# A two-block transformer step in fp32: cross attention and mLSTM sums of squares as high and low fp32r products of a pair added on VectorE

## The chip, the cores and the metric

The program runs on one NeuronCore of a Trainium2 chip. The metric is device time in microseconds (us) for one launch, input and output transfers between the chip's memory and the core included. Three runs of the kernel before gave 1216.65, 1218.11 and 1218.13 us; the median, 1218.11 us, is the time before.

## The reference

Two blocks, batch 1, 256 tokens, width 1024, all in fp32. The first block has three branches on one normalised input: a stick-breaking attention with 8 heads of 128, an mLSTM with 4 heads of 256 (short causal convolution, SiLU, a gated linear recurrence in parallel form), and a cross attention with 4 heads of 256 against 256 memory tokens. Gates mix them, then comes a ReLU-squared MLP. The second block has dilated attention, an SSM and another MLP. The two pieces of it that the change touches are root-mean-square norms over one head's 256 channels:

```
def _rmsnorm(x, g):
    xf = x.astype(jnp.float32)
    y = xf * lax.rsqrt(jnp.mean(xf * xf, axis=-1, keepdims=True) + EPS)
    return (y * g.astype(jnp.float32)).astype(x.dtype)

# cross attention, per head of 256
qn = _rmsnorm(q, gq); kn = _rmsnorm(mk, gk)
# mLSTM, per head of 256
hm = _rmsnorm(hm, ml_norm_g[l].reshape(ML_HEADS, 1, ML_HD))
y_ml = (_merge_heads(hm) * jax.nn.sigmoid(ml_o.astype(jnp.float32))).astype(dt)
```

## The kernel before

Activations lie turned: channels in the 128 partitions, the 256 tokens in the free dimension. All weights (over 200 MB) stream from memory once, in *units* of 1024 x 256. A unit's raw fp32 tile has one of three slots. ScalarE (ACT) rounds it to a high half `w_hi` (L203), VectorE (DVE) subtracts to get the low half `w_lo` (L209), and TensorE (PE) multiplies in the one-pass format fp32r: high by high, high by low, low by high (L241), 48 products of 128x128 by 128x256 for a unit, 24 for each half of its outputs. A unit can't begin on PE before its `w_lo` is written (semaphore `w_split`), and `w_hi` of a slot can't be overwritten before PE has finished the unit that was there.

There is no scheduler. The order of work on each engine is written out by hand, engine by engine, and each engine runs its instructions strictly in that order, with waits on semaphores between engines. So the attention work of a head (the "thread" of small operations) is interleaved by hand with the units.

A head of 256 channels is two tiles. Its sum of squares over channels is a sum over partitions, taken by PE as a product of a 128x128 matrix of ones with the squares, which puts the sum in every partition. These products are plain fp32 (through `mm`, L1618). In the profile one fp32 product shows as two records.

*Cross attention* has four heads. In pass i (1 to 4) PE computes the first half of the key unit, then `cross_sums` for head i-1, then the second half, half the query unit, `cross_logits`, and so on. `c_sq` holds four tiles of squares, two of k and two of q, written by ACT (L520 for k, L540 for q). DVE adds each pair into one tile (`cross_pair`, L1098); PE makes one fp32 product with ones for k and one for q; ACT turns the sums into inverse roots (`inv_rms`, L445 and L446), DVE scales (L1110), PE makes the logits.

*mLSTM* has four heads, and for i = 1 to 3 a pass of four units q, k, v, o. On PE: unit q, scores of head i-1, unit k, half of unit v, values of head i-1, the other half, half of unit o, `mlstm_sums` of head i-1 (two fp32 products with ones, one for each tile of squares), the other half of unit o. ACT runs, in this order: the square of the head's output (L637), `inv_rms` on the sums (L445, L446), the copy of unit v out of PSUM (L455), a table load and the SiLU of the *next* head (L621), the `w_hi` of a unit (L203), the sigmoid gate (L642), a table load (L450), the output's high half (L647), the copy of unit o, another `w_hi`. DVE runs: two `w_lo`, the divide of head i-1 (L1225 to L1229), the convolution of head i (L1198, three groups of four operations, each group waiting for the one before), the scaling with the inverse root (L1235), a `w_lo`, the gate product (L1241), the output's low half (L992), a `w_lo`, the decay weights and scores of head i (L1211 to L1219), a copy of unit k (L982). The fourth head's small operations lie among the units of the stage that follows, `gx` (eight units, L690 its gates).

Chains between the engines that matter below: DVE's convolution, then ACT's SiLU, then ACT's `w_hi`, then DVE's `w_lo`, then the next PE unit.

Of the kernel before, what the change touches and what calls it, by code (L numbers as in the profile page):

```python
# [8 lines left out]
FP32 = mybir.dt.float32  # L9
FP32R = mybir.dt.float32r  # L10
ALU = mybir.AluOpType
ACT = mybir.ActivationFunctionType
AXX = mybir.AxisListType.X

P = 128
T = 256
# [37 lines left out]
H0, M0, Y0 = 0, 8, 16  # L54
H2, M2 = M0, H0
YSB, YML, YX = Y0, Y0 + 8, Y0 + 16
# [41 lines left out]
def build(nc, a, out):  # L98

    ctx = ExitStack()  # L100
    with ctx:
# [5 lines left out]
        def S(name):  # L107
            if name not in sems:
                sems[name] = ctx.enter_context(nc.semaphore(name))
            return sems[name]  # L110
# [6 lines left out]
        x_hi = sb("x_hi", [P, OPND, T], FP32R)  # L117
        x_lo = sb("x_lo", [P, OPND, T], FP32R)
# [3 lines left out]
        ident, ones, later = (cst[:, n * P:(n + 1) * P] for n in range(3))  # L122
# [21 lines left out]
        def bank(b, *dims):  # L144
            v = ps[:, b, :]
            if len(dims) == 3:
                return v[:, 0:dims[0] * dims[1] * dims[2]].rearrange("p (a b c) -> p a b c", a=dims[0], b=dims[1])
            if len(dims) == 2:
                return v[:, 0:dims[0] * dims[1]].rearrange("p (a b) -> p a b", a=dims[0])
            return v[:, 0:dims[0]]  # L150
# [5 lines left out]
        def rows(t, at, n):  # L156
            return t[:, at:at + n, :]

        def need(eng, name, n):

            if n > 0:
# [10 lines left out]
        n_hi, n_lo = (v[:, M0:M0 + 3, :].rearrange("p a b -> p (a b)").rearrange("p (h c) -> p h c", h=2)  # L172
                      for v in (x_hi, x_lo))
        ones_r, later_r = (x_hi[:, M0 + 3, n * P:(n + 1) * P] for n in range(2))
        dtc, acs = (small[:, n:n + 64].rearrange("p (t h) -> p t h", t=2) for n in (256, 320))
        skip = tab[:, 40 * KT:40 * KT + 16]
        dtb, a_log = (tab[0:32, n:n + 1] for n in (40 * KT + 16, 40 * KT + 17))
# [127 lines left out]
        def conv_tiles(i):  # L305
            return [2 * i, 2 * i + 1, 2 * i + 8, 2 * i + 9]
# [131 lines left out]
        def _(act):  # L438
            ahead = iter(range(len(FILLED)))
            chain = Chain(act, S("act_chain"))  # L440
# [30 lines left out]
            def early_hi(u):  # L471

                next(ahead)
                for n in (0, 4):
                    act.wait_ge(S(f"w_early{u}_{n}"), 16)
                    A(w_hi[:, u, n:n + 4], raw[:, u, n:n + 4], ACT.Copy)\
                        .then_inc(S(f"w_hi{u}_half" if n == 0 else f"w_hi{u}"), 1)
# [9 lines left out]
                A(rows(x_hi, H0 + 2 * b, 2), mix[:, 2 * b:2 * b + 2], ACT.Copy).then_inc(S("xn_hi"), 1)  # L487

            early_hi(0)
            act.wait_ge(S("eps"), 1)  # L490
            act.wait_ge(S("mem_ss"), 1)
            inv_rms(mem_row, bank(6, T), D).then_inc(S("mem_rs"), 1)
# [476 lines left out]
        def _(dve):  # L969
# [125 lines left out]
            def cross_pair(j, n):  # L1095

                dve.wait_ge(S("c_sq"), 2 * j + n + 1)
                tt(c_sq[:, 2 * n], c_sq[:, 2 * n], c_sq[:, 2 * n + 1], ALU.add).then_inc(S("c_pair"), 1)  # L1098

            cross_pair(0, 0)  # L1100

# [87 lines left out]
                low(2 * (i - 1) + YSB, bank(7, 2, T), "y_hi", i + 4, "y_lo")  # L1189


            def conv(pad, dst, name, tiles, stride):

                for m in range(1, 4):
                    if m > 1:
                        chain(last)
                    for n in range(4):
                        last = stt(dst[:, n], pad[:, n, m:m + T], pc("conv_w" + name, tiles[n] + stride * m),  # L1198
                                   dst[:, n], ALU.mult, ALU.add)
                return last  # L1200

            def mlstm_conv(i):

                dve.wait_ge(S("rnn_c0"), i + 1)
                conv(m_qkp, m_cv, "", conv_tiles(i), 16).then_inc(S("rnn_cv"), 1)

            def mlstm_weights(j):

# [63 lines left out]
            def gated(stage, i, first, n=None, splits=2):  # L1272

                for _ in range(splits):
                    split()
                u = U(stage, i, 1, 2)
                dst = rows(mix, 2 * i, 2)
                evacuated(dve, u - 1)
                finished(dve, u)
                tt(gt, gt, unit_bank(u), ALU.mult).then_inc(taken(u), 1)  # L1280
                evacuated(dve, u)
                if first:
                    V.tensor_copy(dst, gt).then_inc(S("p_used"), 1)
                else:
                    tt(dst, dst, gt, ALU.add).then_inc(S("p_used"), 1)
                if n is not None:
                    low(2 * i + M0, dst, "mix_hi", n, "mix_lo")
# [3 lines left out]
            mlstm_scores(3)  # L1291
            gated("gx", 1, True)
            mlstm_divide(3)
            gated("gx", 2, True)
            mlstm_scale(3)
            mlstm_gate(3)
            gated("gx", 3, True)
# [316 lines left out]
        def _(pe):  # L1614
            FP, TOK = False, True

            def mm(o, l, r, start=True, stop=True):
                return nc.tensor.matmul(o, l, r, start=start, stop=stop)  # L1618
# [9 lines left out]
            def half(u, o, at, tok=FP, nk=KT, lo=None):  # L1628

                if o == 0:  # L1630
                    begin(u)
                last = products(pe, u, o, at, tok, nk, lo=lo)
                if o == 1:
                    last.then_inc(S(f"unit{u % SLOTS}"), 1)

            def unit(u, at, tok=FP, nk=KT, lo=None):
                half(u, 0, at, tok, nk, lo)
                half(u, 1, at, tok, nk)
# [76 lines left out]
            def cross_sums(j):  # L1715

                pe.wait_ge(S("c_pair"), 2 * j + 2)
                for n in range(2):
                    last = mm(bank(3, 2, T)[:, n], ones, c_sq[:, 2 * n])
                last.then_inc(S("c_ss"), 1)  # L1720

            def cross_logits(j):
# [22 lines left out]
                last.then_inc(S("soft_y"), 1)  # L1745

            pe.wait_ge(S("cst_in"), 16)
            for i in range(1, 5):
                k, q, v = (U("cross", i, n, 3) for n in range(3))
                mem, x = (M0, YSB) if i < 4 else (H0, H0)  # L1750
                if i == 4:
                    pe.wait_ge(S("xn_lo"), 4)
                half(k, 0, mem)
                cross_sums(i - 1)
                if i == 4:
                    gate_sums()
                half(k, 1, mem)
                half(q, 0, x)
                cross_logits(i - 1)
                half(q, 1, x)  # L1760
                half(v, 0, mem, TOK)
                cross_turn(i - 1)
                half(v, 1, mem, TOK)
                if i == 4:
                    gate_columns()
                cross_values(i - 1)
# [62 lines left out]

            def mlstm_sums(j):  # L1830

                pe.wait_ge(S("rnn_sq"), j + 1)
                for d in range(2):
                    last = mm(bank(6, T), ones, m_sq[:, d], d == 0, d == 1)
                last.then_inc(S("rnn_ss"), 1)

            q, k, v, o = (U("mlstm", 0, n, 4) for n in range(4))
            half(q, 0, H0)
# [7 lines left out]
            for i in range(1, 4):  # L1846
                q, k, v, o = (U("mlstm", i, n, 4) for n in range(4))
                unit(q, H0)
                mlstm_scores(i - 1)
                unit(k, H0)  # L1850
                half(v, 0, H0, TOK)
                mlstm_values(i - 1)
                half(v, 1, H0, TOK)
                half(o, 0, H0)
                mlstm_sums(i - 1)
                half(o, 1, H0)

            def gated(stage, i, at, nk=KT, h=H0):

                unit(U(stage, i, 0, 2), h)  # L1860
                unit(U(stage, i, 1, 2), at, FP, nk)
# [330 lines left out]
```

## Time and profile before

| what | value |
|---|---|
| median of three runs | 1218.11 us (1216.65 to 1218.13) |
| the profiled execution's own time | 1217.88 us |
| its span, first to last instruction | 1216.1 us |
| PE busy | 1203.7 us, 99% |
| DVE busy | 814.0 us, 67% |
| ACT busy | 672.5 us, 55% |
| mean data rate from memory | 173 GB/s |
| cross attention passes on PE | about 30 to 124 us |
| mLSTM passes on PE | about 186 to 296 us, `gx` to about 347 us |

Matmuls overlap in the records, so that a product's own duration is longer than the step from one to the next. The time that a product costs PE is read from the starts of the records. A busy share near 100% says that PE seldom stops; it doesn't say that nothing else decides where it stops. For that there is the chain of waits, which follows the work that ended last back from its end.

### The profile page before, as it was taken

What the parts mean: (1) busy time and instruction counts of PE and PEld (TensorE: products, weight loads), DVE (VectorE), ACT (ScalarE), POOL (GpSimd) and SP (SyncE); (2) the same over time, 40 slices, a digit from 0 to 9 for tenths busy, and PEclk for the clock granted to TensorE, in tenths of its full rate; (3) what the DMA queues carried; (4) which work ended last, traced back from release to release, by engine and by line L of the source; (5) the groups of instructions that cost most, each with busy time, mean ns of one, the idle gap of its engine ahead of it and who ended that gap; (6) DMA issues with size and microseconds to landing.
All of it is one profiled execution on the core that took longest, in us unless ns stands there. A gap on an engine that the chain in (4) does not pass through costs nothing.

```text
span 1216.1 us, 21663 instructions
## 1 busy us (share of the span) xinstructions
PE 1203.7 (99%) x9458; PEld 1169.4 (96%) x9458; DVE 814.0 (67%) x913; ACT 672.5 (55%) x801; POOL 11.0 (1%) x24
## 2 busy tenths in 40 slices
PE   9999999999999999999999999999999999999998
PEld 8999999999999999999999999999999998999886
DVE  7866676777655566776447658888885457777543
ACT  7643545676544444554344558889876345555442
POOL 0000000000000000000000000000000000000000
PEclk9999999999999999999999999999999999999999
DMA  9543445555655554556565546556455564455651
GB/s 326 171 157 105 143 151 163 152 148 158 193 184 183 179 170 156 179 193 218 174 190 179 177 129 202 174 171 194 148 176 163 191 208 139 156 174 181 235 190 53
DMA packets 202494, 210.75 MB, mean 173 GB/s; under 512 B 6540, under 2 KB 191244, under 8 KB 202400
## 3 DMA queue, kind: packets, MB, share of 16 engines
q1 hardware_dynamic: 199712, 200.30, 51.9%
q0 software_dynamic: 2112, 8.17, 2.4%
q8 instruction: 75, 1.23, 0.4%
q10 hardware_dynamic: 576, 0.90, 0.2%
q14 instruction: 19, 0.16, 0.0%
HBM read 208.25 MB, written 1.09 MB: 172 GB/s over the span
## 4 chain that ended last, share of the span: by engine, by line
PE 91%; DVE 4%; ACT 4%; DMA 1%; issue 1%; DVEq 0%; ACTq 0%
PE ps L241 73%; PE ps L2111 7%; PE ps L1618 6%; DVE w_lo L209 2%; PE ps L1667 1%; ACT w_hi L203 1%; PE ps L1621 1%; DVE arena L1198 1%; PE ps L2071 1%; PE ps L250 1%; DMA arena<-rows 0%; DMA pcol<-in_params 0%; PE ps L2078 0%; ACT L642 0%; DVE arena L1227 0%
## 5 line engine op out<-in xcount | busy, mean ns | idle before, releaser
L241 PE MATMUL ps<-x_hi,w_hi 128*128 128x256 f32 x2448 | 702.2, 287 | 0.5 <-DVE w_lo L209 0.4
L241 PE MATMUL ps<-x_hi,w_lo 128*128 128x256 f32 x2448 | 692.6, 283 | 0.0
L241 PE MATMUL ps<-x_lo,w_hi 128*128 128x256 f32 x2448 | 692.5, 283 | 0.0
L209 DVE TENSOR_TENSOR w_lo<-raw,w_hi 128x2048 fp32r<-128x2048 f32 x187 | 427.5, 2291 | 228.9 <-ACT w_hi L203 228.9
L241 PEld LDWEIGHTS ps<-x_hi,w_hi 128*128 128x128 f32 x2448 | 469.4, 192 | 4.9 <-issue 3.4
L241 PEld LDWEIGHTS ps<-x_lo,w_hi 128*128 128x128 f32 x2448 | 469.5, 192 | 0.8
L241 PEld LDWEIGHTS ps<-x_hi,w_lo 128*128 128x128 f32 x2448 | 469.3, 192 | 0.0
L203 ACT CAST w_hi<-raw 128x2048 fp32r<-128x2048 f32 x187 | 354.3, 1900 | 118.1 <-PE ps L241 73.8
L1618 PE MATMUL ps<-arena 128*128 128x256 f32 (+5 forms) x432 | 66.0, 340 | 1.3 <-ACT arena L843 1.3
L241 PE MATMUL ps<-w_hi,x_hi 128*128 128x256 f32 x224 | 64.3, 287 | 0.0
L241 PE MATMUL ps<-w_lo,x_hi 128*128 128x256 f32 x224 | 63.3, 283 | 0.0
L241 PE MATMUL ps<-w_hi,x_lo 128*128 128x256 f32 x224 | 63.3, 283 | 0.0
L1198 DVE SCALAR_TENSOR_TENSOR arena<-arena,pcol 128x256 f32<-128x256 f32 x144 | 60.2, 480 | 3.5 <-ACT arena L607 2.7
L1618 PEld LDWEIGHTS ps<-arena 128*128 128x128 f32 (+2 forms) x432 | 52.9, 170 | 8.5 <-ACT arena L843 1.5
L764 ACT ACTIVATE arena<-ps 128x512 f32<-128x512 f32 x30 | 17.9, 598 | 77.6 <-PE ps L241 77.6
L2111 PE MATMUL ps<-w_hi,x_hi 128*128 128x512 f32 x128 | 49.8, 389 | 0.0
L2111 PE MATMUL ps<-w_hi,x_lo 128*128 128x512 f32 x128 | 49.8, 389 | 0.0
L2111 PE MATMUL ps<-w_lo,x_hi 128*128 128x512 f32 x128 | 49.8, 389 | 0.0
L1356 DVE TENSOR_TENSOR arena<-arena 128x512 f32<-128x512 f32 x32 | 22.1, 692 | 31.9 <-ACT arena L764 31.9
L241 PEld LDWEIGHTS ps<-w_hi,x_lo 128*128 128x128 f32 x224 | 42.9, 191 | 0.0
L241 PEld LDWEIGHTS ps<-w_hi,x_hi 128*128 128x128 f32 x224 | 42.9, 191 | 0.0
L241 PEld LDWEIGHTS ps<-w_lo,x_hi 128*128 128x128 f32 x224 | 42.9, 191 | 0.0
(233 smaller groups left out, 960.3 us busy)
## 6 DMA issues: line engine op xcount, KB each, us to landing
raw<-in_w_in SPq DMA_DIRECT2D x170, 512.0 KB, 4.6
raw<-in_w_ff SPq DMA_DIRECT2D x64, 512.0 KB, 4.5
raw<-in_w_up SPq DMA_DIRECT2D x32, 512.0 KB, 4.7
raw<-in_w_down SPq DMA_DIRECT2D x32, 512.0 KB, 4.4
raw<-in_w_mem_kv SPq DMA_DIRECT2D x16, 512.0 KB, 5.7
raw<-in_w_out SPq DMA_DIRECT2D x16, 512.0 KB, 4.9
raw<-in_w_ssm_proj SPq DMA_DIRECT2D x16, 512.0 KB, 4.7
raw<-in_w_x_proj SPq DMA_DIRECT2D x8, 512.0 KB, 4.6
```

The costliest lines, as they stand in the source:

```text
L203: nc.scalar.copy(w_hi[:, s], raw[:, s]).then_inc(S(f"w_hi{s}"), 1)
L209: nc.vector.tensor_tensor(w_lo[:, s], raw[:, s], w_hi[:, s].bitcast(FP32), ALU.subtract)\
L241: last = nc.tensor.matmul(dst, l, r, start=start and k == 0 and m == 0, stop=stop and k == nk - 1 and m == 2)
L250: last = nc.tensor.matmul(dst, wt[:, c], xt[:, at + k, :], start=k == 0 and m == 0, stop=k == KT - 1 and m == 2)
L764: A(f, unit_bank(u), ACT.Relu).then_inc(taken(u), 1)
L1198: last = stt(dst[:, n], pad[:, n, m:m + T], pc("conv_w" + name, tiles[n] + stride * m), dst[:, n], ALU.mult, ALU.add)
L1356: chain(tt(q, f, bc(rs_row(), 2), ALU.mult))
L1618: return nc.tensor.matmul(o, l, r, start=start, stop=stop)
L1621: return nc.tensor.transpose(o, i, ident[0:i.shape[0], 0:i.shape[0]])
L1667: last = nc.tensor.matmul(dst, l, r, start=kind == 0 and k == 0, stop=kind == 2 and k == KT - 1)
L2071: nc.tensor.matmul(dst, wt[:, u % SLOTS, k, o * P:(o + 1) * P], x_hi[:, H0 + k, :], start=k == 0 and m == 0, stop=False)
L2111: last = nc.tensor.matmul(y_bank(c, t), xt[:, U0 + 4 * (b % 8) + k, t * P:(t + 1) * P], wide(wt[:, u % SLOTS])[:, k], start=b % 8 == 0 and ...
```

## The change

In both places DVE now produces one tile for a pair of squares and splits it into an fp32r high half and an fp32r low half, kept in rows of `x_hi` and `x_lo` that are free at that time, and PE multiplies each half with ones in fp32r.

- Cross attention: `cross_pair` has three dependent operations (add, cast, subtract) where it had one. `cross_sums` has four fp32r products where it had two fp32 ones. The ones in fp32r are written by ACT near the program's start.
- mLSTM: a new `mlstm_pair` (add, cast, subtract) on DVE, placed between the first and the second group of the next head's convolution; for the fourth head it stands between the two `w_lo` of the third pair of `gx`. `mlstm_sums` has two fp32r products where it had two fp32 ones, and stands behind the whole unit o, where it stood between its halves.

```diff
+        c_hi, c_lo = (rows(v, YML, 2) for v in (x_hi, x_lo))
+        m_hi, m_lo = (v[:, M0 + 4, :] for v in (x_hi, x_lo))
+        ones_c = x_hi[:, YML + 4, 0:P]
...
             early_hi(0)
+            act.wait_ge(S("ones"), 1)
+            A(ones_c, ones, ACT.Copy).then_inc(S("ones_c"), 1)
...
             def cross_pair(j, n):
                 dve.wait_ge(S("c_sq"), 2 * j + n + 1)
-                tt(c_sq[:, 2 * n], c_sq[:, 2 * n], c_sq[:, 2 * n + 1], ALU.add).then_inc(S("c_pair"), 1)
+                chain(tt(c_sq[:, 2 * n], c_sq[:, 2 * n], c_sq[:, 2 * n + 1], ALU.add))
+                chain(V.tensor_copy(c_hi[:, n], c_sq[:, 2 * n]))
+                tt(c_lo[:, n], c_sq[:, 2 * n], c_hi[:, n].bitcast(FP32), ALU.subtract).then_inc(S("c_pair"), 1)
...
-            def conv(pad, dst, name, tiles, stride):
+            def conv(pad, dst, name, tiles, stride, between=None):
                 for m in range(1, 4):
                     if m > 1:
                         chain(last)
+                    if m == 2 and between is not None:
+                        between()
...
+            def mlstm_pair(j):
+                dve.wait_ge(S("rnn_sq"), j + 1)
+                chain(tt(m_sq[:, 0], m_sq[:, 0], m_sq[:, 1], ALU.add))
+                chain(V.tensor_copy(m_hi, m_sq[:, 0]))
+                tt(m_lo, m_sq[:, 0], m_hi.bitcast(FP32), ALU.subtract).then_inc(S("m_pair"), 1)
...
-                conv(m_qkp, m_cv, "", conv_tiles(i), 16).then_inc(S("rnn_cv"), 1)
+                conv(m_qkp, m_cv, "", conv_tiles(i), 16, (lambda: mlstm_pair(i - 1)) if i else None)\
+                    .then_inc(S("rnn_cv"), 1)
...
             mlstm_divide(3)
-            gated("gx", 2, True)
+            split()
+            mlstm_pair(3)
+            gated("gx", 2, True, splits=1)
...
                 pe.wait_ge(S("c_pair"), 2 * j + 2)
                 for n in range(2):
-                    last = mm(bank(3, 2, T)[:, n], ones, c_sq[:, 2 * n])
+                    mm(bank(3, 2, T)[:, n], ones_c, c_hi[:, n], True, False)
+                    last = mm(bank(3, 2, T)[:, n], ones_c, c_lo[:, n], False, True)
                 last.then_inc(S("c_ss"), 1)
...
             def mlstm_sums(j):
-                pe.wait_ge(S("rnn_sq"), j + 1)
-                for d in range(2):
-                    last = mm(bank(6, T), ones, m_sq[:, d], d == 0, d == 1)
-                last.then_inc(S("rnn_ss"), 1)
+                pe.wait_ge(S("m_pair"), j + 1)
+                mm(bank(6, T), ones_r, m_hi, True, False)
+                mm(bank(6, T), ones_r, m_lo, False, True).then_inc(S("rnn_ss"), 1)
...
                 half(v, 1, H0, TOK)
-                half(o, 0, H0)
+                unit(o, H0)
                 mlstm_sums(i - 1)
-                half(o, 1, H0)
```

On DVE, in the first mLSTM pass, from the divide to the scaling, the instructions stand like this in the kernel before (`arena` is the scratch tile, `pcol` holds the convolution's weights, the waits are semaphores):

```order
L1229 TENSOR_TENSOR arena<-ps,arena 128x512 [waits rnn_num,dve_chain]
L1198 SCALAR_TENSOR_TENSOR arena<-arena,pcol 128x256 [waits rnn_c0]
L1198 SCALAR_TENSOR_TENSOR arena<-arena,pcol 128x256 x3
L1198 SCALAR_TENSOR_TENSOR arena<-arena,pcol 128x256 [waits dve_chain]
L1198 SCALAR_TENSOR_TENSOR arena<-arena,pcol 128x256 x3
L1198 SCALAR_TENSOR_TENSOR arena<-arena,pcol 128x256 [waits dve_chain]
L1198 SCALAR_TENSOR_TENSOR arena<-arena,pcol 128x256 x3
L1235 SCALAR_TENSOR_TENSOR arena<-arena,pcol 128x256 [waits rnn_r]
```

The same stretch of DVE in the changed kernel, whose line numbers are a little higher:

```order
L1246 TENSOR_TENSOR arena<-ps,arena 128x512 [waits rnn_num,dve_chain]
L1207 SCALAR_TENSOR_TENSOR arena<-arena,pcol 128x256 [waits rnn_c0]
L1207 SCALAR_TENSOR_TENSOR arena<-arena,pcol 128x256 x3
L1214 TENSOR_TENSOR arena<-arena 128x256 [waits rnn_sq,dve_chain]
L1215 CAST x_hi<-arena 128x256 [waits dve_chain]
L1216 TENSOR_TENSOR x_lo<-arena,x_hi 128x256 [waits dve_chain]
L1207 SCALAR_TENSOR_TENSOR arena<-arena,pcol 128x256 x4
L1207 SCALAR_TENSOR_TENSOR arena<-arena,pcol 128x256 [waits dve_chain]
L1207 SCALAR_TENSOR_TENSOR arena<-arena,pcol 128x256 x3
L1252 SCALAR_TENSOR_TENSOR arena<-arena,pcol 128x256 [waits rnn_r]
```

The add, the cast and the subtract stand between the first and the second group, and each of the three waits for the one before it. The second group waits for nothing new, but stands behind them in the queue.

On DVE, in the first cross attention pass, between the q tile's pair and the logits' reduction, the changed kernel has these rows (before, the first three were one `TENSOR_TENSOR`, L1098):

```order
L1103 TENSOR_TENSOR arena<-arena 128x256 [waits c_sq]
L1104 CAST x_hi<-arena 128x256 [waits dve_chain]
L1105 TENSOR_TENSOR x_lo<-arena,x_hi 128x256 [waits dve_chain]
L212 TENSOR_TENSOR w_lo<-raw,w_hi 128x2048 [waits w_hi1]
L212 TENSOR_TENSOR w_lo<-raw,w_hi 128x2048 [waits w_hi2]
L1117 SCALAR_TENSOR_TENSOR arena<-arena,pcol 128x256 [waits c_r]
```

Two `w_lo` and the scaling for the logits are behind the longer pair.

## Rows read from the trace of the kernel before

**Rows 1.** The page's first part: busy time, share and instructions by engine.
```profile
PE 1203.7 (99%) x9458; PEld 1169.4 (96%) x9458; DVE 814.0 (67%) x913; ACT 672.5 (55%) x801; POOL 11.0 (1%) x24
```
**Rows 2.** Chain that ended last, mLSTM stage: start us, us, what.
```profile
237.02 0.88 PE ps L1618 x4
...
263.42 1.59 DVE arena L1198 x4
...
266.74 1.69 DVE arena L1198 x4
...
294.56 1.68 DVE arena L1198 x4
...
306.95 2.30 DVE w_lo L209
309.39 11.74 PE ps L241 x96
...
335.48 115.19 PE ps L241 x960
```
**Rows 3.** Timeline of PE, second cross pass: start us, us, engine, line, what.
```profile
54.63 1.03 PE L1618 MATMUL ps<-arena,cst 128*128 128x256 f32 x4
55.31 0.47 PE L241 MATMUL ps<-x_hi,w_hi 128*128 128x256 f32 x1
55.62 0.28 PE L241 MATMUL ps<-x_lo,w_hi 128*128 128x256 f32 x1
```
**Rows 4.** DVE's copies into tile mix: line, count, duration ns min/median/max.
```profile
L1283 DVE COPY mix<-arena x8: 427/427/428, 313.8 to 930.1; 128x512 f32<-128x512 f32 x8
```
**Rows 5.** Timeline of DVE, first and second cross pass.
```profile
31.02 0.84 DVE L1098 TENSOR_TENSOR arena<-arena 128x256 f32<-128x256 f32 x2
...
36.18 1.67 DVE L1110 SCALAR_TENSOR_TENSOR arena<-arena,pcol 128x256 f32<-128x256 f32 x4
...
53.84 0.42 DVE L1098 TENSOR_TENSOR arena<-arena 128x256 f32<-128x256 f32 x1 [0.56 <-ACT arena L540]
```
**Rows 6.** Timeline of PE, first cross pass: the sums, then the logits.
```profile
32.63 1.03 PE L1618 MATMUL ps<-arena,cst 128*128 128x256 f32 x4
...
39.24 1.89 PE L1618 MATMUL ps<-arena 128*128 128x256 f32 x8
```
**Rows 7.** Timeline of PE, mLSTM: first sums, next key unit, third sums.
```profile
236.86 1.03 PE L1618 MATMUL ps<-arena,cst 128*128 128x256 f32 x4
...
247.58 0.36 PE L241 MATMUL ps<-x_hi,w_hi 128*128 128x256 f32 x1
...
291.95 1.13 PE L1618 MATMUL ps<-arena,cst 128*128 128x256 f32 x4 [0.40 <-ACT arena L637]
```
**Rows 8.** Timeline of ACT, first mLSTM pass, from the norm to the SiLU.
```profile
237.93 0.47 ACT L445 ACTIVATE arena<-ps,small 128x256 f32<-128x256 f32 x1 [2.40 <-PE ps L1618]
...
239.36 1.28 ACT L621 ACT_TABLE_LOAD   x1
240.65 1.06 ACT L621 ACTIVATE arena<-arena 128x1024 f32<-128x1024 f32 x1
```
**Rows 9.** Timeline of DVE, mLSTM passes.
```profile
231.47 0.42 DVE L1225 SCALAR_TENSOR_TENSOR arena<-ps,arena 128x256 f32<-128x256 f32 x1
231.93 0.42 DVE L1226 TENSOR_TENSOR arena<-arena,ps 128x256 f32<-128x256 f32 x1
...
243.61 2.29 DVE L209 TENSOR_TENSOR w_lo<-raw,w_hi 128x2048 fp32r<-128x2048 f32 x1 [2.96 <-ACT w_hi L203]
...
263.34 5.08 DVE L1198 SCALAR_TENSOR_TENSOR arena<-arena,pcol 128x256 f32<-128x256 f32 x12
```
**Rows 10.** PE's waits: line, for whom, us in total, times, longest.
```profile
PE ps L2071 <- ACT x_hi L939: 2.9, 1, 2.9
```
**Rows 11.** Busy time after that wait: window, PE, PEld, DVE, ACT, POOL, granted clock, DMA share, GB/s.
```profile
1026.00:1030.00 4.00, 3.74 (x19) 3.77 (x20) 4.00 (x12) 3.08 (x7) 0.00 (x0) 0.58 0.09 30
```
**Rows 12.** Chain that ended last, same place: start us, us, what.
```profile
1026.26 3.41 PE ps L2071 x16
```

More of the change, by code:

```diff
@@ L1747, in _ @@
             pe.wait_ge(S("cst_in"), 16)
+            pe.wait_ge(S("ones_c"), 1)
             for i in range(1, 5):
```

## The prediction

> **What bounds the kernel now.** I read the page's first part first: PE is busy 99% of the span [rows 1]. That says PE is the bound, so work taken off PE should shorten the kernel. Then the chain of waits, in order of time, over the stages that the change touches. In the cross attention it runs on PE without a break. In the mLSTM stage it doesn't: it leaves PE at the first head's sums, at 237.02, and comes back at 309.39, when PE takes up a unit whose `w_lo` DVE finished at 306.95 + 2.30 = 309.25. For 72 us it goes through ACT and DVE alone, over the convolutions (four of the second head's operations at 263.42 and four at 266.74, and four of the third's at 294.56) [rows 2]. PE looks busy there because it runs just ahead of its inputs; DVE and ACT set the pace. So the change has to be read twice, once as work taken from PE, once as work put on a chain that already ends last.
>
> **What PE gains.** An fp32r product costs PE 115.19 / 960 = 0.120 us [rows 2]. The two fp32 products of the cross sums show as four records; the first starts at 54.63, and the two products of weights after them at 55.31 and 55.62. Without the sums these two would start at 54.63 and 54.75. So the two fp32 products cost 55.62 - 54.75 = 0.87 us [rows 3]. Four fp32r products cost 0.48, two cost 0.24. The gain is 0.39 us at each of the four cross sums and 0.63 at each of the four mLSTM sums: 4.1 us together, if nothing is late.
>
> **What an added pair costs DVE.** An add or a subtract of 128x256 takes 0.42, and a dependent operation starts 0.04 after the end of the one before (231.47 + 0.42 to 231.93) [rows 9]. No cast between two SBUF tiles stands in DVE's trace. Nearest: a copy of 128x512 takes 0.427 [rows 4], as long as a tensor-tensor operation on half the elements. A tensor-tensor operation takes 2.29 for 2048 elements and 0.42 for 256 [rows 9], that is 1.04 ns an element and 0.155 us fixed. A copy at twice that rate takes 0.155 + 256 x 0.52 ns = 0.29 us for 256. The other end is a cast at the single rate, 0.42. I take 0.29, since the form is nearest to the copy. The Trainium skill ("Vector Engine (DVE) Microarchitecture Reference", section 5.1, Performance modes) lists cast beside copy among the operations that run at double rate from SBUF to SBUF; by that rule the cast is at the low end; no row here shows whether an fp32r output keeps it, and if the rule fails the sum below comes out 0.9 us higher. So the add's result is ready, then cast and subtract take 0.04 + 0.29 + 0.04 + 0.42 = 0.79 us more. In DVE's queue the next operation need not wait for the subtract's end to start, so three operations hold it for about 1.17 us (0.46 + 0.33 + 0.38).
>
> **Cross attention, passes 2 to 4.** The k pair has long been added; the q pair waits for ACT's square and its add starts at 53.84 and ends at 54.26 [rows 5]. PE's sums start at 54.63 [rows 3]. A hand-over from DVE to PE takes 0.14 (309.25 to 309.39) [rows 2], so the slack is 0.23 us. The pair gets 0.79 longer: PE waits 0.56, against 0.39 gained. Each pass loses 0.17 us, three lose 0.5.
>
> **Cross attention, first pass.** Here both pairs follow each other from 31.02 [rows 5]. The second subtract ends at 31.02 + 1.17 + 1.21 = 33.40; PE can start at 33.54 where it started at 32.63 [rows 6]. It loses 0.91 - 0.39 = 0.52 us. Behind the pairs on DVE stand two `w_lo` and the scaling, which starts at 36.18 and takes 1.67 [rows 5]. It comes 1.54 later and ends at 39.39; the logits stand at 39.24 [rows 6] + 0.52 = 39.76. That costs nothing, with 0.2 to spare. The copy of the ones on ACT near the start I cost at nothing: the only thing behind it that is near is a half of `w_hi` that waits for its DMA, and if that cover were gone it would be its own 0.3 us. Cross attention altogether: 0.5 + 0.5 = +1.0 us. With a hand-over of nothing it is +0.5, with a cast of 0.42 it is +1.7.
>
> **mLSTM, first pass.** The first sums move behind the whole unit o, half a unit or 24 x 0.12 = 2.88 us later, and are 0.63 shorter. ACT's norm waits for them (it starts at 237.93, released by PE) and with it everything in ACT's queue behind it: the copy of unit v, the table load that ends where the SiLU starts (240.65), then the `w_hi` [rows 8]. The norm now starts 2.88 - 0.63 = 2.25 later. DVE's longer convolution is hidden under that. So the chain is 2.25 us late when it reaches the next `w_lo`, which ended at 243.61 + 2.29 = 245.90 [rows 9]. PE took up that unit at 247.58 [rows 7]. It had 1.54 us in hand after a hand-over; now it is 0.63 early and the `w_lo` 2.25 late, so that PE waits 1.3 us.
>
> **mLSTM, second and third pass.** The pair stands inside the convolution, and the convolution is on the chain: each adds 1.17. Is the norm worse still? The second convolution starts at 263.34 [rows 9] + 2.25 = 265.59. Its first group takes 1.69, the pair 1.21: sums ready at 268.49, on PE at 268.63. Two products later, 0.45 us, the norm starts at 269.08, and from norm to the end of the table load ACT takes 240.65 - 237.93 = 2.72 [rows 8]: 271.80. The convolution itself ends at 265.59 + 5.08 + 1.17 = 271.84. The two ways tie, and the pass costs 1.17, not more. PE waits at the sums too (before, the third waited 0.40 for ACT's square [rows 7]), but such a wait no longer shows where the `w_lo` is later still.
>
> **Sum.** At the unit that PE took up at 309.39 the `w_lo` is 2.25 + 2 x 1.17 = 4.6 us late. Everything that PE gained at three sums before it is waited away. The fourth head's sums stand behind the third pair of `gx`, far from any wait, and keep their 0.63. So mLSTM gives +4.0 us, cross attention +1.0, together +5.0. On the profiled execution's own 1217.88 (1.8 us outside its span of 1216.1) that is 1222.9; the median of the runs is 0.2 above that execution, so I predict 1223.0 us. Behind `gx` nothing is changed and PE keeps its distance. The terms at their ends: 4.4 us with hand-overs of nothing, 5.9 with the slow cast, so 1222.3 to 1224.0 for this case alone.
>
> **Rivals.**
> - *PE's work decides, as its 99% say.* Then the 4.1 us come out, and the old waits at the mLSTM sums (0.40 at the third [rows 7]) go with them: 1217.9 - 4.1 - 0.4 = 1213.4 us. It needs the chain through ACT and DVE to have over 4 us to spare, where the row at 309.39 shows it released PE. 6%.
> - *The late norm is absorbed.* If a wait of ACT or DVE on something timed by PE lies between the norm and the next pass, the 2.25 us vanish, and only the two convolutions stay: 2.3 - 0.63 + 1.0 = +2.7, and with cross attention at its low end +2.2: 1220.3 to 1220.8. Against it: the chain passes from the first sums to 309.39 without PE. 12%.
> - *The clock.* In the second pair of units of `gx` PE now stands still for about 2.6 us at one time (4.6 late plus 0.6 early, less what was waited before in that pass). The one wait of that length before, 2.9 us [rows 10], was followed by a mean granted clock of 0.58 over four us [rows 11], so a part at 1.2 GHz and the rest at 2.4, and 16 products then took 3.41 us where 16 x 0.12 = 1.92 would do [rows 12]: 1.5 us lost. The Trainium skill ("TensorE: Matmul & The Clock Gate", What's actually happening) says that the clock falls to half after idling, and the trace agrees there. After a shorter wait it need not fall. If it does: 1224.5. 12%.
> - *The split doesn't pay but doesn't harm.* Small covers that I have missed at each place bring it to no change, 1218 us. 6%.
>
> **Chances.** The forecast has 64%. A measurement of this kernel tells about 0.2%, or 2.4 us, from no change: the bounds are 1215.7 and 1220.5. Faster: the first rival, 6%. Within: the last rival and half of the second, 12%. Slower: the rest, 82%. For eight in ten the range goes from 1220.0, which holds most of the absorbed norm, to 1226.0, which holds the slow cast and the clock's fall together.
>
> **What would show it.** PE's records at the first `gx` units: a wait on `w_lo` of over 2 us. The `w_lo` that ended at 245.90 ending at about 249.1 (2.25 and the cross attention's 1.0 later), and PE released by it. The third convolution's last group, at 294.56 before [rows 2], starting 2.25 + 2 x 1.17 + 1.0 = 5.6 us later. Waits of 0.5 us for DVE's subtract at the cross sums, 0.9 at the first. The cast at 0.29 or 0.42. A norm of the first head that starts early or a `gx` without waits would refute the steps for mLSTM, and a shorter span than before the whole.

## The result

| | before | after |
|---|---|---|
| median | 1218.13 us (1216.65 to 1219.13, 7 runs) | 1222.37 us (1221.68 to 1224.95, 7 runs) |
| profiled execution, its span | 1217.88, 1216.1 us | 1222.14, 1220.3 us |

The ratio is 1.0038, with a 95% interval of 1.0026 to 1.0050: the kernel is 4.2 us slower. 1223.0 was forecast.

The page's first part of the changed kernel. PE is busy for 2.1 us less than in [rows 1] and DVE for 9.4 us more with 28 more operations, and the span is 4.2 us longer:

```profile
PE 1201.6 (98%) x9450; PEld 1166.8 (96%) x9450; DVE 823.4 (67%) x941; ACT 672.5 (55%) x802; POOL 11.0 (1%) x24
```

The longest waits of PE in the changed kernel (line, for whom, us in total, times, longest). In the kernel before, PE waited for a `w_lo` once, 0.4 us:

```profile
PE ps L244 <- DVE w_lo L212: 4.6, 3, 2.4
PE ps L2090 <- ACT x_hi L944: 2.9, 1, 2.9
PE ps L1637 <- DVE x_lo L1105: 1.6, 4, 0.6
...
PE ps L1637 <- DVE x_lo L1216: 0.9, 2, 0.5
```

The first row is units that wait for their low half in the mLSTM passes and at the second `gx` unit. The third is the four cross sums, which wait for the subtract; the last is the mLSTM sums of the second and third pass, which do too. The second was there before [rows 10].

The chain that ended last, in the same stage as [rows 2] (start us, us, what):

```profile
241.31 0.48 ACT arena L448
...
244.03 1.06 ACT arena L626
...
266.80 1.59 DVE arena L1207 x4
269.68 0.52 PE ps L1637 x2
270.22 0.48 ACT arena L448
...
295.71 1.59 DVE arena L1207 x4
297.32 0.44 DVE arena L1214
298.59 0.52 PE ps L1637 x2
...
304.81 2.30 DVE w_lo L212
307.25 7.38 PE ps L244 x48
```

Before, the second and third pass went through the last group of the convolution into the SiLU. Now they go through its first group, the pair, the sums on PE (L1637) and the norm (L448). The forecast had these two ways end within 0.04 us of each other. In the trace they end closer still. In the second pass the longer convolution is done at 269.54 + 3.37 = 272.91, the table load behind the norm at 271.64 + 1.28 = 272.92, and the SiLU starts at 272.94 (timelines of DVE and ACT):

```profile
269.54 3.37 DVE L1207 SCALAR_TENSOR_TENSOR arena<-arena,pcol 128x256 f32<-128x256 f32 x8
```
```profile
271.64 1.28 ACT L626 ACT_TABLE_LOAD   x1
272.94 1.06 ACT L626 ACTIVATE arena<-arena 128x1024 f32<-128x1024 f32 x1
```

How late each place is, against the kernel before, from the records' starts and ends in the two timelines:

| place | `w_lo` late | PE late |
|---|---|---|
| first unit behind the first cross sums | | 0.57 |
| first unit of the mLSTM stage | 1.12 | 1.12 |
| second unit of the second pass, behind the first norm | 3.37 | 1.83 |
| second unit of the third pass | 4.50 | 3.39 |
| second unit of `gx` | 5.59 | 5.59 |
| third unit of `gx` | 5.59 | 6.30 |
| first unit behind `gx` | 5.70 | 5.70 |
| first MLP to the end of the gates of the second block | 5.7 | 5.7 |
| behind the wait before the second MLP | 4.3 | 4.3 |

Two jumps have nothing to do with the edit's instructions: 0.7 us at the third `gx` unit, where PE is late and its `w_lo` isn't, and 1.5 us given back before the second MLP, which the kernel before loses there in its profile and this one doesn't. Both are the clock's, below.

### The profile page after: what moved, and what is told of

Same layout as the page of the kernel before. It is cut to its first block, busy times and chain, and to the rows that moved or that the text cites. A ratio compares the mean times of both kernels' runs of the same rounds, so it can differ in the third digit from the quotient of the medians.

```text
span 1220.3 us, 21680 instructions
## 1 busy us (share of the span) xinstructions
PE 1201.6 (98%) x9450; PEld 1166.8 (96%) x9450; DVE 823.4 (67%) x941; ACT 672.5 (55%) x802; POOL 11.0 (1%) x24
## 3 DMA queue, kind: packets, MB, share of 16 engines
HBM read 208.25 MB, written 1.09 MB: 172 GB/s over the span
## 4 chain that ended last, share of the span: by engine, by line
PE 90%; ACT 4%; DVE 4%; DMA 1%; issue 1%; DVEq 0%; ACTq 0%
PE ps L244 72%; PE ps L2130 7%; PE ps L1637 6%; DVE w_lo L212 2%; PE ps L1686 1%; ACT w_hi L206 1%; PE ps L1640 1%; PE ps L253 1%; PE ps L2090 1%; DMA arena<-rows 0%; DMA pcol<-in_params 0%; ACT L626 0%; PE ps L2097 0%; DVE arena L1244 0%; DVE arena L1207 0%
## 5 line engine op out<-in xcount | busy, mean ns | idle before, releaser
L1637 PE MATMUL ps<-arena 128*128 128x256 f32 (+5 forms) x432 | 66.0, 340 | 1.3 <-ACT arena L848 1.3
L1637 PEld LDWEIGHTS ps<-arena 128*128 128x128 f32 (+2 forms) x432 | 52.9, 170 | 8.6 <-ACT arena L848 1.5
L695 ACT ACTIVATE arena<-ps,pcol 128x256 f32<-128x256 f32 x40 | 16.8, 471 | 47.8 <-PE ps L244 47.8
```

The costliest lines, as they stand in the source:

```text
L695: last = A(gt[:, c], unit_bank(u)[:, c], ACT.Sigmoid, bias=pc(b_gate, k + c))
```

## The experiments

All medians are beside runs of the kernel before on the same chip: 1218.24 us for e1 to e4, 1218.23 for e5 to e8, 1218.0 for e9 to e12. "Late" is against the profiled execution of the kernel before. The starts of two executions of one kernel differ by some 0.1 us (0.07 in e12), and nothing is made of differences that small.

**e1, the cross attention part alone.** The kernel before with the new `cross_pair` and `cross_sums`:

```diff
+                chain(tt(c_sq[:, 2 * n], c_sq[:, 2 * n], c_sq[:, 2 * n + 1], ALU.add))
+                chain(V.tensor_copy(c_hi[:, n], c_sq[:, 2 * n]))
+                tt(c_lo[:, n], c_sq[:, 2 * n], c_hi[:, n].bitcast(FP32), ALU.subtract).then_inc(S("c_pair"), 1)
```

> Only the cross attention part of the change; mLSTM as before. Theory (the longer pair on DVE is waited for by PE): PE waits about 0.9 us for the subtract at the first cross sums and 0.55 at each of the three others, against 0.39 us gained at each, so the unit that follows the last cross sums is 1.1 us late and the whole is +1.1 us, about 1219.2. Rival (PE's work decides): 4 x 0.39 = 1.6 us faster, about 1216.5.

Measured: 1219.19 us (1217.62 to 1219.63, 10 runs), ratio 1.0008 (0.9998 to 1.0017). By time alone that is at the edge of what can be told. The trace tells it: PE is 1.03 us late at the first mLSTM unit and still at the first unit behind `gx`. Its waits:

```profile
PE ps L1633 <- DVE x_lo L1104: 1.6, 4, 0.6
```

These are four waits where there were none. What the saved products gain is less than what the later start costs.

**e2, the mLSTM part alone.**

```diff
+                conv(m_qkp, m_cv, "", conv_tiles(i), 16, (lambda: mlstm_pair(i - 1)) if i else None)\
...
+                unit(o, H0)
                 mlstm_sums(i - 1)
```

> Only the mLSTM part of the change; cross attention as before. Theory (the chain through ACT and DVE is 2.25 us late by the moved sums and 1.1 late by each of two longer convolutions): the w_lo of the second gx unit ends 4.5 us later than in the kernel before, PE waits 2.4 to 2.7 us for it, and the whole is +3.9 us, up to +4.7 if the granted clock falls after that wait: 1222.0 to 1222.8. Rival (PE's work decides): 4 x 0.63 and the old waits, 3 us faster.

Measured: 1221.32 us (1221.11 to 1224.23, 6 runs), ratio 1.0030 (1.0018 to 1.0043). The `w_lo` of the second `gx` unit, in this kernel and in the kernel before (timeline of DVE: start us, us, engine, line, what):

```profile
303.83 2.29 DVE L210 TENSOR_TENSOR w_lo<-raw,w_hi 128x2048 fp32r<-128x2048 f32 x1 [2.20 <-ACT w_hi L204]
```
```profile
299.22 2.29 DVE L209 TENSOR_TENSOR w_lo<-raw,w_hi 128x2048 fp32r<-128x2048 f32 x1 [2.19 <-ACT w_hi L203]
```

4.6 us late, where 4.5 was expected. Behind `gx` PE is 4.74 late. The expectation of a time near 1222.0 was 0.7 too high: in this trace the clock holds behind the wait before the second MLP (1.00 over 1031 to 1035 us), where the kernel before loses 1.5 us [rows 11 and 12], and PE is only 3.43 late behind it. Five of the six times lie within 0.3 us of the profiled one.

**e3, the whole pair, but the sums between the halves of unit o.**

```diff
                 half(o, 0, H0)
                 mlstm_sums(i - 1)
                 half(o, 1, H0)
```

> As e2, but the mLSTM sums stand between the halves of unit o, as in the kernel before. Theory: the first norm waits for the subtract alone (0.35 us later than before), the first SiLU for the longer convolution (+0.4), and each further pass adds 1.1: the w_lo of the second gx unit ends 2.6 us late, and the whole is +2.0 us, 1.9 less than e2: about 1220.2. PE waits at the sums for DVE's subtract about 0.9 us in each of the three passes, in place of waits at the units. Rival (the place of the sums doesn't matter, since the convolution decides): as e2.

Measured: 1221.27 us (1220.27 to 1221.65, 8 runs), ratio 1.0024 (1.0014 to 1.0035). Half right. The same `w_lo`:

```profile
301.86 2.29 DVE L210 TENSOR_TENSOR w_lo<-raw,w_hi 128x2048 fp32r<-128x2048 f32 x1 [2.19 <-ACT w_hi L204]
```

2.64 us late (2.6 expected), 2.0 less than in e2: so the place of the sums is worth 2 us on the chain. But the whole is 3.0 above before, not 2.0. I had PE wait 0.9 us at each sums; it waits 2.1 in the second and the third pass, since it is early there and the pair isn't:

```profile
266.71 0.39 PE L1631 MATMUL ps<-x_hi 128*128 128x256 f32 x1 [2.15 <-DVE x_lo L1210]
```

and behind the third such wait the granted clock is 0.66 over five us (window, PE, PEld, DVE, ACT, POOL, granted clock, DMA share, GB/s):

```profile
295.00:300.00 5.00, 4.36 (x24) 4.36 (x25) 4.60 (x12) 3.75 (x6) 0.00 (x0) 0.66 0.31 83
```

PE takes up the third `gx` unit 3.70 us late and its `w_lo` was ready 2.64 late: the clock cost 1.1 us here, the miss.

**e4, the move alone.** fp32 sums of two squares as before, no pair, but behind unit o:

```diff
-                half(o, 0, H0)
+                unit(o, H0)
                 mlstm_sums(i - 1)
-                half(o, 1, H0)
```

> The kernel before with one edit: its fp32 mLSTM sums of two squares, without any pair on DVE, stand behind the whole unit o. Theory: the first norm is 2.88 us late; in the second and third pass the norm, not the convolution, holds the SiLU, since it waits for PE, which itself waits for the late w_lo; each pass adds about 0.95: the w_lo of the second gx unit ends 4.8 us late, the whole +4.8 us, about 1223. Rival (only DVE's added work costs): no change, 1218.

Measured: 1223.16 us (1222.19 to 1225.04, 4 runs), ratio 1.0043 (1.0028 to 1.0058). The strongest single result: an edit that adds no instruction anywhere, and moves two products by 2.9 us, costs as much as the whole change. The times spread with the clock (two of the four are at 1222.2 and 1222.3, the profiled one is 1225.04), so the lateness of the `w_lo` is the better witness. It is 4.9 us:

```profile
304.14 2.29 DVE L209 TENSOR_TENSOR w_lo<-raw,w_hi 128x2048 fp32r<-128x2048 f32 x1 [3.20 <-ACT w_hi L203]
```

and in the second pass the norm waits for PE (timeline of ACT), 4.35 us later than the same norm of the kernel before, which started at 265.31:

```profile
269.66 0.48 ACT L445 ACTIVATE arena<-ps,small 128x256 f32<-128x256 f32 x1 [2.66 <-PE ps L1618]
...
272.38 1.06 ACT L621 ACTIVATE arena<-arena 128x1024 f32<-128x1024 f32 x1
```

The SiLU of the next head stands behind that norm in ACT's queue, and with it a `w_hi` that PE needs.

**e5, the pair's work twice.** As e2, and in the first three passes, inside the convolution:

```diff
+                if j < 3:
+                    spare = cells(3856, T)
+                    chain(tt(spare, m_sq[:, 0], m_hi.bitcast(FP32), ALU.subtract))
+                    chain(V.tensor_copy(spare, m_sq[:, 0]))
+                    chain(tt(spare, m_sq[:, 0], m_hi.bitcast(FP32), ALU.subtract))
```

> As e2, and in the first three mLSTM passes DVE does the pair's work a second time (a subtract, a copy, a subtract, each waiting for the one before, results unused) inside the convolution: 1.25 us more in each. Theory (the added DVE work is on the chain in the second and third pass, and hidden behind the late norm in the first): the w_lo behind the first pass is as late as in e2 (+2.4), the one behind the second 3.5 + 1.25 = 4.7, the second gx unit's 4.6 + 2.5 = 7.1 us late; the whole 2.5 above e2, about 1223.9. Rival (DVE has room, the place of the sums is all): as e2, 1221.3.

Measured: 1225.45 us (1223.37 to 1226.52, 4 runs), ratio 1.0056 (1.0042 to 1.0069). The `w_lo` behind the first pass is 2.3 us late as in e2, so there the added work is hidden behind the late norm. The next is 4.7 late and this one 7.05 (7.1 expected):

```profile
306.27 2.29 DVE L210 TENSOR_TENSOR w_lo<-raw,w_hi 128x2048 fp32r<-128x2048 f32 x1 [2.20 <-ACT w_hi L204]
```

DVE's work counts in full in the second and third pass, and not at all in the first. The time is 1.5 us above what I expected. The traces say where that comes from. Behind `gx` this kernel is 7.24 late against 4.74 in e2, the 2.5 that were expected. But the sum stood on e2, whose trace keeps the clock before the second MLP, and this one's doesn't (windows of e2 and of this kernel, each from about where PE starts again behind the wait):

```profile
1031.00:1035.00 4.00, 3.82 (x32) 3.85 (x33) 4.00 (x12) 3.02 (x7) 0.00 (x0) 1.00 0.06 19
```
```profile
1033.00:1037.00 4.00, 3.40 (x16) 3.43 (x17) 4.00 (x12) 3.25 (x7) 0.00 (x0) 0.57 0.18 60
```

**e6, PE kept busy in its longest new wait.** The changed kernel, with products that nobody uses:

```diff
                 unit(U(stage, i, 0, 2), h)
+                if stage == "gx" and i == 0:
+                    for _ in range(10):
+                        mm(bank(7, P), ones, ones)
```

> The changed kernel, and between the first and the second gx unit PE makes ten fp32 products of ones with ones (128x128, about 0.2 us each, result unused), so that it stands still for some 0.3 us instead of 2.4 to 2.7. Theory (the clock fell there because PE stood still; by itself that costs 0.7 us of the delay behind gx): no fall of the granted clock near 307 us, the second gx unit starts when its w_lo is there, 5.6 us later than before, and the third waits for its w_lo again, also 5.6 late, not 6.3; the whole some 0.7 us below the changed kernel where that had the fall: about 1221.7. Rival (the clock falls by chance, whatever PE does): the fall is there as before, 6.3.

In the changed kernel PE waits 2.42 us for the second `gx` unit, and the products behind the wait are 0.21 us apart where 0.12 is usual (307.61 to 307.82), so at the 1.2 GHz level; over four us the granted clock is 0.57:

```profile
307.25 0.55 PE L244 MATMUL ps<-x_hi,w_hi 128*128 128x256 f32 x1 [2.42 <-DVE w_lo L212]
307.61 0.41 PE L244 MATMUL ps<-x_lo,w_hi 128*128 128x256 f32 x1
307.82 0.41 PE L244 MATMUL ps<-x_hi,w_lo 128*128 128x256 f32 x1
```
```profile
307.00:311.00 4.00, 3.75 (x20) 3.78 (x21) 2.29 (x6) 3.25 (x6) 0.00 (x0) 0.57 0.70 211
```

With the filler the wait is 0.17 us, and the granted clock stays at 1.00, the 2.4 GHz level:

```profile
304.79 2.40 PE L1637 MATMUL ps<-cst 128*128 128x128 f32 x20
307.36 0.36 PE L244 MATMUL ps<-x_hi,w_hi 128*128 128x256 f32 x1 [0.17 <-DVE w_lo L212]
```
```profile
307.00:311.00 4.00, 3.83 (x32) 3.67 (x31) 2.40 (x6) 3.26 (x6) 0.00 (x0) 1.00 0.65 194
```

The third `gx` unit is 5.71 us late, not 6.30: standing still cost 0.6 us, less than the 1.4 us that slow products lose from the start of this unit to its end (5.59 late to 6.99), because PE was waiting for the next `w_lo` anyway. The time didn't follow, a miss: 1223.36 us (1221.99 to 1224.42, 4 runs), ratio 1.0043 (1.0028 to 1.0059), against 1222.37 for the changed kernel. The trace shows one reason. Behind `gx` PE is 5.09 late, where it was 5.70; from about 747 us on it is 5.55, where it was 5.75. PE waits there in the second block for ACT, and ACT for a transfer, longer in this execution than in that of the changed kernel (timelines of ACT, changed kernel first):

```profile
744.14 2.88 ACT L860 ACTIVATE mix<-arena,small 128x256 f32<-128x256 f32 x8 [0.59 <-DMA arena<-rows]
```
```profile
743.94 2.90 ACT L860 ACTIVATE mix<-arena,small 128x256 f32<-128x256 f32 x8 [0.93 <-DMA arena<-rows]
```

How long this wait is differs by execution, filler or not: e9, which up to there is the kernel before, leaves it 0.25 us later than that kernel's profile. The profiled execution of e6 is only 0.15 us below the changed kernel's (1221.99 against 1222.14). The other three, which have no trace, show a lower mean clock (0.997 and 0.998 against 0.999). That the filler holds the clock in `gx` is shown; that it makes the kernel faster isn't, and e10, which has a second filler too, doesn't part the two.

**e7, high and low halves only where nothing waits.** The k tile of the second to fourth head, and the fourth head's mLSTM sums; all else as before:

```diff
+                if n or not j:
+                    tt(c_sq[:, 2 * n], c_sq[:, 2 * n], c_sq[:, 2 * n + 1], ALU.add).then_inc(S("c_pair"), 1)
+                    return
...
+                if j < 3:
+                    pe.wait_ge(S("rnn_sq"), j + 1)
+                    for d in range(2):
+                        last = mm(bank(6, T), ones, m_sq[:, d], d == 0, d == 1)
```

> The kernel before, with high and low fp32r sums only where DVE's longer pair is hidden: the k tile of the cross sums of the second to fourth head, and the fourth head's mLSTM sums behind the third pair of gx. The q tile, the first head and the other mLSTM sums are as before. Theory: 3 x 0.19 + 0.63 = 1.2 us faster, no new wait on PE, about 1217.0. Rival (the k pair delays something on DVE that PE waits for): waits on PE at the cross sums, no gain.

Measured: 1217.11 us (1215.55 to 1218.46, 11 runs), ratio 0.9991 (0.9982 to 1.0000). PE is 0.53 us early at the first mLSTM unit (3 x 0.19 is 0.57) and 1.09 early behind `gx`. In the second cross pass the sums start without a wait and take 0.68 us where they took 0.87:

```profile
54.68 0.28 PE L1639 MATMUL ps<-x_hi 128*128 128x256 f32 x1
54.80 0.28 PE L1639 MATMUL ps<-x_lo,x_hi 128*128 128x256 f32 x1
54.92 0.60 PE L1639 MATMUL ps<-arena,cst 128*128 128x256 f32 x2
```

By time alone the 1.1 us are at the edge of what can be told; the trace tells it. Where DVE's longer pair is off the chain, the work saved is worth its price on PE.

**e8, e7 and a filler before the second MLP.** In its profile the kernel before loses its clock at the 2.9 us wait there [rows 10 to 12].

```diff
+            for _ in range(12):
+                mm(bank(6, P), ones, ones)
             first = [(U("up2", n), o, first_banks(U("up2", n))[o]) for n in range(2) for o in range(2)]
```

> As e7, and twelve fp32 products of ones with ones on PE (result unused) in the 2.9 us in which it waits for the first high half of the second MLP. Theory (standing still lets the clock fall in most executions of the kernel before, and the fall costs 1.5 us): no fall near 1027 us, the stretch behind the wait at 0.12 us a product, 1.2 to 1.5 us less than e7: about 1215.6. Rival (the filler delays the start, or the clock falls in any case): as e7 or 0.5 us above it.

Measured: 1215.58 us (1215.26 to 1215.90, 10 runs), ratio 0.9978 (0.9968 to 0.9987), faster than the kernel before. The wait is 0.23 us, and the window behind it has the full clock:

```profile
1022.36 2.84 PE L1639 MATMUL ps<-cst 128*128 128x128 f32 x24
1025.44 0.35 PE L2104 MATMUL ps<-x_hi,w_hi 128*128 128x256 f32 x1 [0.23 <-ACT x_hi L944]
```
```profile
1024.00:1028.00 4.00, 3.77 (x32) 3.60 (x32) 4.00 (x13) 2.57 (x6) 0.00 (x0) 1.00 0.39 134
```

Ten runs lie within 0.64 us, where 20 of the kernel before lie within 3.6. Most of that kernel's spread goes with the clock: of its 55 executions beside the experiments, nine have a mean granted clock of 0.999 and take 1216.7 to 1217.0 us, 36 have 0.998 and take 1217.7 to 1218.7, ten have 0.997 or less and take 1219.1 to 1220.2.

**e9 and e10, both kernels with a steady clock.** The kernel before with e8's filler; the changed kernel with e6's and e8's.

> The kernel before with the twelve filler products of e8 before the second MLP (result unused). Theory: no fall of the granted clock in the middle of the span, 1216.7 us (e8's 1215.6 plus the 1.1 of e7), with a spread under 1 us. Rival (the falls come by chance): a median of 1218.

> The changed kernel with both fillers, that of e6 in gx and that of e8 before the second MLP. Theory: what the change costs apart from the clock is 1.1 in cross attention plus 4.5 at the second gx unit less 0.6 at the fourth sums, 5.0 us, so 1221.7 against e9's 1216.7. Waits of 1.2 us at two mLSTM units are left, after which the clock may still fall in some executions. Rival (the change's own cost is smaller, and the clock makes up the rest): under 1220.5.

Measured: 1216.68 us (1216.38 to 1216.97, 10 runs), ratio 0.9990 (0.9981 to 1.0000), and 1221.57 us (1221.31 to 1221.92, 7 runs), ratio 1.0029 (1.0018 to 1.0040). Both as expected, and the ranges are under 0.7 us. The difference is 4.89 us: what the change costs where neither kernel loses the clock behind these waits. The forecast's sum was 5.0. In the trace of e10 PE is 4.94 late behind `gx`.

**e11 and e12, both kernels once more.**

> The changed kernel once more, for where its clock falls in another execution. Theory: the w_lo of the second gx unit 5.6 late as before, whatever the clock does; a fall in the waits before the second gx unit or before the second MLP, or at both.

> The kernel before once more, for where its clock falls in another execution. Theory: a fall at the wait before the second MLP or none; none in the mLSTM passes or in gx, where its longest wait is 0.7 us.

One execution each: 1225.06 and 1218.06 us. In e11 the `w_lo` of the second `gx` unit is 5.57 late, as in the first profile (5.59). The clock falls behind the wait in `gx` again, and this time before the second MLP too, where PE goes from 6.14 late to 7.15 late:

```profile
1032.00:1036.00 4.00, 3.59 (x17) 3.63 (x18) 4.00 (x12) 3.23 (x7) 0.00 (x0) 0.50 0.11 36
```

In the first profile of the changed kernel the same window, behind that same wait, had the full clock:

```profile
1032.00:1036.00 4.00, 3.99 (x33) 4.00 (x34) 4.00 (x12) 2.98 (x6) 0.00 (x0) 1.00 0.04 13
```

So a wait of the same 2.9 us is followed by a fall in one execution and not in another. e12 has the fall before the second MLP and none in `gx`.

## Why the prediction was right, point by point

- *PE isn't what decides in the mLSTM stage.* Right. PE is busy 2.1 us less and the kernel is slower; e4 slows it by 4.9 with no work added.
- *The gain on PE.* Right: two fp32r products take 0.24 us (240.87 to 241.11), and the fourth mLSTM sums gave 0.62 (6.32 late before them, 5.70 behind).
- *The cast at 0.29.* Right, 0.294 for all twelve, the length worked out for the double rate, so an fp32r output keeps it here. The Trainium skill ("Vector Engine (DVE) Microarchitecture Reference", section 5.1, Performance modes) lists cast among the operations that run at double rate from SBUF to SBUF. The trace agrees with the 0.294.

```profile
L1104 DVE CAST x_hi<-arena x8: 293/294/294, 31.6 to 99.3; 128x256 fp32r<-128x256 f32 x8
L1215 DVE CAST x_hi<-arena x4: 293/294/295, 238.1 to 337.2; 128x256 fp32r<-128x256 f32 x4
```

- *Cross attention, first pass +0.52, then +0.17 each.* Right: 0.57, 0.18, 0.20 and 0.18 (0.09 of the first was there before the sums, so 0.48 is its own). In the second pass the operations stand as worked out: add, cast, subtract without a gap, and the sums 0.05 us behind, so the hand-over was smaller than the 0.14 taken:

```profile
54.41 0.42 DVE L1103 TENSOR_TENSOR arena<-arena 128x256 f32<-128x256 f32 x1 [0.56 <-ACT arena L545]
54.87 0.29 DVE L1104 CAST x_hi<-arena 128x256 fp32r<-128x256 f32 x1
55.20 0.42 DVE L1105 TENSOR_TENSOR x_lo<-arena,x_hi 128x256 fp32r<-128x256 f32 x1
```
```profile
55.67 0.39 PE L1637 MATMUL ps<-x_hi 128*128 128x256 f32 x1 [0.31 <-DVE x_lo L1105]
```

- *The first norm 2.25 late.* Right: 3.37 less the 1.12 from before is 2.25. e3 takes that term away (the same `w_lo` is 0.39 late there). e4 shows the move alone, 2.92 late, since its sums are not 0.63 shorter.
- *Each longer convolution 1.17.* Right in size, 1.13 and 1.09 a pass. As to the way, the chain names the pair, the sums and the norm, and the convolution ends 0.01 us before the table load, so that the tie worked out in the forecast is there and neither way alone is the cause. e5 doubles the term.
- *The `w_lo` in `gx` 4.6 late.* Right: 5.59 less 1.12 is 4.47. The forecast put it at the unit that PE took up at 309.39, which is the third of `gx`; the long wait of 2.42 us came one unit earlier, at the second, whose `w_lo` is as late.
- *The sum.* 1218.11 and 5.0 make 1223.1 and not 1223.0, a slip that changes nothing. *Behind `gx` PE keeps its distance* holds in the changed kernel's profile (5.70 to 5.75 until the second MLP), but in e6's execution a wait near 747 us takes back 0.4 of the 0.6 that the filler had gained.
- *The clock.* Given 12%, as a rival. It happened in both profiles of the changed kernel, and in those of e2, e4 and e5, so it was underrated. Its price was overrated: I said 1.5 us on top; behind `gx` it was 0.7, because 0.7 us of waiting for the next `w_lo` covered the rest. And I had treated the fall before the second MLP as fixed, where in the kernel before it is most of the difference between executions. In the profile the two effects leave 0.8 us less (0.7 more behind `gx`, 1.5 less at the second MLP), and so the median came 0.6 us under the forecast: 4.24 us slower as measured, 4.89 with the clock held in both. The sum of the mechanism, 5.0, is borne out by the 4.89; that the median lands where it does is in part luck with the clock. How often each fall comes in the changed kernel is open, with two profiles of it.
- *Where the e3 expectation failed*, it left out the clock, and in its waits another thing: a wait's length on PE is the lateness of its releaser plus what PE has gained since it last waited, and I left out the second term.

## What to carry to other kernels

A PE that is busy 99% of the span can still run just ahead of a chain through other engines. In such a stage of this kernel work saved on PE turned into waiting. An operation put on that chain came out of the time in full (e5, second and third pass), one beside it not at all (e5, first pass), and a result that PE hands over later delayed all that stands behind it in the other engine's queue (e4). So before moving work off the "bound" engine, follow the chain of waits through the stage, and use the edit only where it doesn't pass (e7). A filler in a long wait of PE held the clock in every trace that has one (e6, e8, e9, e10). It made the times steadier in e8, e9 and e10; in e6, alone in `gx`, it didn't.

## What the runs showed of the hardware that was not expected

A wait of 2.9 us before the second MLP is followed by the lower clock in some executions of one kernel and not in others. In the changed kernel the mean over 1032 to 1036 us is 1.00 in the first profile and 0.50 in the second; over all kernels without a filler there, eight traces have the fall and three don't. The wait of 2.4 us at the second `gx` unit is followed by a fall in all five traces that have it (the changed kernel twice, e2, e4, e5), with a mean of 0.57 to 0.73 over four us. The two waits of 1.1 us in the passes of the changed kernel are followed by none (1.00 over 249 to 253 and over 278 to 282 us). Of e3's two waits of about 2.1 us one is followed by a fall (0.66) and one isn't (1.00 over 266 to 271 us). What decides whether a given wait is followed by a fall is not shown. Twelve products whose result nobody reads, in the 2.9 us wait, shrank the range of the runs from 2.6 us (16 runs) to 0.6 (10 runs) and the median by 1.3 us (1218.0 to 1216.68).
